# First MLP: relu transposed by VectorE blocks and ScalarE quarter copies, GpSimd issues the modulation pieces; both MLPs take the relu behind the fifth split

## The chip, the cores and the metric

The kernel runs on one core of a Trainium2 chip. The metric is the device time of one execution in microseconds. Before the change the median of three runs is 2226.82 us (2226.66 to 2227.34). Engines: TensorE (PE, with PEld for its weight loads), VectorE (DVE), ScalarE (ACT), GpSimd (POOL), SyncE (SP).

## The reference

Two transformer layers over a sequence of 256 tokens, model width 2048, in float32. Layer 0 mixes tokens by differential attention, layer 1 by sliding-window attention; each is followed by a squared-ReLU MLP of width 8192. Scale, shift and gate of each of the four sub-layers are computed from one conditioning vector c.

```python
def squared_relu_mlp(h, w_up, w_down):
    return jnp.square(jax.nn.relu(h @ w_up)) @ w_down

    c_act = jax.nn.silu(c)
    for i in range(DEPTH):
        mod = (c_act @ w_ada[i] + b_ada[i])[:, None, :]
        sh_a, sc_a, g_a, sh_m, sc_m, g_m = jnp.split(mod, N_MOD, axis=-1)
        h = x * (1.0 + sc_a) + sh_a
        ...
        x = layer_norm(ALPHA * x + (1.0 + g_a) * y, ln_mix_g[i], ln_mix_b[i])
        h = x * (1.0 + sc_m) + sh_m
        y = squared_relu_mlp(h, w_up[i], w_down[i])
        x = layer_norm(ALPHA * x + (1.0 + g_m) * y, ln_mlp_g[i], ln_mlp_b[i])
```

## The kernel before

**Blocks, subtiles, splits.** All weights are streamed once. A block is one product of 256 tokens by a 2048 x 512 piece of weights. SP loads it in four quarters of 1 MB into five slots `raw`. A block is worked off in 8 subtiles of 256 weight rows each. For a subtile ScalarE rounds the weights to float32r (`w_hi`, L528, `split_hi`), VectorE takes the rest (`w_lo = raw - w_hi`, L901, `split_lo`, written over `raw`), and TensorE does 12 matmuls: w_hi with the high part of the activations, w_lo with the high part, w_hi with the low part (L1709 to L1711), into `pair[:, b % 2]` in PSUM. Work on one subtile's weights by ScalarE and VectorE is called split n here, n from 0 to 7. `w_hi` has 6 slots, so split n of a block waits until TensorE has finished the subtile six before it (`used`); `pair` has two halves, so a block's result must have left PSUM before the second block after it starts.

**The MLPs.** Each MLP is four quarters of the width of 8192. A quarter is four up blocks (h into 512 columns each of w_up, with relu and square behind them) and four down blocks (f into w_down, added up in `y`); 32 blocks in each MLP. The order on each engine is written out by hand: `block_` runs over the 8 splits and calls at given numbers what else stands beside them: `before` (behind split `at`), `later` (behind its split), `hooks` and, on VectorE, `ada_tile` for the pieces. The work on the result of an up block stands in the block behind it, on all engines.

**The relu, its transpose and the square.** An up block's result has tokens on the partitions, the down product needs features there. In the first MLP ScalarE takes the relu from PSUM into `R` behind split 1 (`up_relu`, L553), TensorE turns `R` with eight transposes into `turn[:, 0]` in PSUM behind its subtile 1 (`turn_up`, `turn_tile`, L1603), ScalarE squares it twice from there behind split 4 (L560 into `SQ`, L561 rounded into `f_hi`), and VectorE takes the rest behind split 4 (`up_lo`, L1031, `f_lo`). In the second MLP (`ON_CHIP`), ScalarE's relu stands behind split 2, VectorE turns `R` with 16 transposes of 32 x 256, eight behind split 2 and eight behind split 3 (`up_turn_half`, L1040), each of which also moves its blocks to other partitions, ScalarE squares twice behind split 5 (L572, L573) and VectorE takes the rest behind split 5 (L1057). The first down block of a quarter waits for three `f_lo` at its start and for the fourth at its subtile 6.

**The modulation.** `c_act @ w_ada` is done on VectorE: a piece is 128 x 1024 of w_ada (0.5 MB), multiplied by one number per partition and added to `acc` (L929; L926 for the first of a sum). 16 pieces make a sum, which TensorE then adds over the partitions (L1627 or L1638). The first MLP carries 192 pieces, six or seven in each of 28 blocks, behind splits 0, 1, 3, (4,) 5, 6, 7 (`MLP_ADA`); the second 32. Pieces have four slots `ada_w`. SP issues them (`load_ada`, L374) between the weight quarters (`load_raw`, L397), in one queue; a piece waits until VectorE has used the one four before it, a quarter until TensorE has used the slot. In the first four blocks behind each norm VectorE also applies the norm's gain and bias to `x` (`affine`, L1311, L1312) behind split 7. GpSimd does the `rstd` powers, and clears `y` before the first block's result is needed (L1581); VectorE waits for that at the start of the MLP's second block.

## Time and profile before

| | |
|---|---|
| median of 3 runs | 2226.82 us (2226.66 to 2227.34) |
| the profiled execution | 2228.67 us, span 2226.9 us |
| TensorE busy | 2168.5 us, 97% of the span, granted clock 0.993 on average |
| VectorE busy | 1790.6 us, 80% |
| ScalarE busy | 981.3 us, 44% |
| GpSimd busy | 33.4 us, 2% |
| chain that ended last | TensorE 88%, VectorE 7% |
| moved by DMA | 596.41 MB, 268 GB/s on average |

The first MLP lies between about 495 and 1226 us of the span, the second between 1502 and the end. Matmuls overlap, so a matmul's own duration (0.39 us) is not its share of the time: their starts stand 0.2265 us apart. In the same way an instruction of ScalarE or VectorE can begin a little before the one in front of it has ended; where a step is spoken of, it is from start to start.

### The profile page before, as it was taken

Reading aid. Unit: us, or ns where it says so; the run is one execution under the profiler, and the core shown is the slowest. Engines: PE = TensorE matmul, PEld = TensorE weight load, DVE = VectorE, ACT = ScalarE, POOL = GpSimd, SP = SyncE. Lnnn points to the kernel's source line nnn. Section 1 sums busy time; section 2 is a strip of 40 time slices with the busy share of each in tenths; the row PEclk is TensorE's granted clock in tenths of the full one; section 3 lists DMA queues with packets and bytes.
Section 4 is the critical chain, followed back from the end, with each engine's and each line's share of the span. In section 5 each row is a group of like instructions: output and inputs, shape, how many; then the busy total and the mean of one; then the engine's idle time right before and its main releaser. Section 6 shows DMA issues by size and latency. Waiting matters only on the chain.

```text
span 2226.9 us, 26022 instructions
## 1 busy us (share of the span) xinstructions
PE 2168.5 (97%) x9952; PEld 1791.8 (80%) x9952; DVE 1790.6 (80%) x2057; ACT 981.3 (44%) x1330; POOL 33.4 (2%) x53
## 2 busy tenths in 40 slices
PE   6999999999999999999999999999999999999997
PEld 6887888877888888888888788777888888888886
DVE  6899998887997897888786888777966865874877
ACT  1135444546433443443353655536534443443441
POOL 0001000000000000000000000000000000000000
PEclk9899999999999999999999999999999999999999
DMA  9999888877999999999985643365766676666663
GB/s 360 384 331 347 322 320 300 306 245 256 361 364 325 354 366 335 325 380 350 323 311 190 198 152 119 122 207 190 236 221 223 213 241 206 219 217 219 228 234 113
DMA packets 262592, 596.41 MB, mean 268 GB/s; under 512 B 13426, under 2 KB 14788, under 8 KB 262468
## 3 DMA queue, kind: packets, MB, share of 16 engines
q1 hardware_dynamic: 254800, 579.45, 74.2%
q10 hardware_dynamic: 7668, 15.30, 2.2%
q8 instruction: 79, 1.29, 0.2%
q14 instruction: 45, 0.37, 0.0%
HBM read 592.60 MB, written 2.10 MB: 267 GB/s over the span
## 4 chain that ended last, share of the span: by engine, by line
PE 88%; DVE 7%; DMA 1%; issue 1%; ACT 1%; SPq 0%; DVEq 0%; POOL 0%; ACTq 0%; POOLq 0%
PE pair L1709 25%; PE pair L1711 25%; PE pair L1710 25%; DVE acc L916 2%; DVE w_lo L901 1%; PE pair L1967 1%; PE pair L1969 1%; PE pair L1968 1%; PE pair L1729 1%; PE pair L1731 1%; PE pair L1730 1%; PE turn L2041 1%; DMA y<-in_w_ada_dram 1%; PE turn L2022 1%; PE turn L1603 1%
## 5 line engine op out<-in xcount | busy, mean ns | idle before, releaser
L528 ACT ACTIVATE w_hi<-raw 128x1024 fp32r<-128x1024 f32 x712 | 726.8, 1056 | 620.2 <-PE pair L1711 297.4
L901 DVE TENSOR_TENSOR w_lo<-raw,w_hi 128x1024 fp32r<-128x1024 f32 x712 | 852.5, 1220 | 117.0 <-ACT w_hi L528 110.8
L1709 PE MATMUL pair<-w_hi,h_hi 128*128 128x512 f32 x1456 | 581.3, 399 | 1.5 <-DVE w_lo L901 0.8
L1711 PE MATMUL pair<-w_hi,h_lo 128*128 128x512 f32 x1456 | 567.8, 390 | 0.0
L1710 PE MATMUL pair<-w_lo,h_hi 128*128 128x512 f32 x1456 | 567.3, 390 | 0.0
L1709 PE MATMUL pair<-w_hi,f_hi 128*128 128x512 f32 x1056 | 414.0, 392 | 0.1
L1711 PE MATMUL pair<-w_hi,f_lo 128*128 128x512 f32 x1056 | 411.1, 389 | 0.0
L1710 PE MATMUL pair<-w_lo,f_hi 128*128 128x512 f32 x1056 | 410.9, 389 | 0.0
L929 DVE SCALAR_TENSOR_TENSOR acc<-ada_w,cvec,acc 128x1024 f32<-128x1024 f32 x300 | 383.6, 1279 | 1.8 <-DVE x L1312 0.9
L1709 PEld LDWEIGHTS pair<-w_hi,h_hi 128*128 128x128 f32 x1456 | 273.5, 188 | 62.9 <-DVE w_lo L901 6.3
L1711 PEld LDWEIGHTS pair<-w_hi,h_lo 128*128 128x128 f32 x1456 | 273.2, 188 | 58.4
L1710 PEld LDWEIGHTS pair<-w_lo,h_hi 128*128 128x128 f32 x1456 | 273.7, 188 | 55.5 <-issue 1.2
L1709 PEld LDWEIGHTS pair<-w_hi,f_hi 128*128 128x128 f32 x1056 | 198.2, 188 | 43.7 <-DVE w_lo L901 2.1
L1710 PEld LDWEIGHTS pair<-w_lo,f_hi 128*128 128x128 f32 x1056 | 198.3, 188 | 41.7 <-issue 1.0
L1711 PEld LDWEIGHTS pair<-w_hi,f_lo 128*128 128x128 f32 x1056 | 198.2, 188 | 41.5
L1040 DVE STREAM_TRANSPOSE work<-work 32x256 f32<-32x256 f32 x256 | 111.6, 436 | 55.7 <-ACT work L553 52.2
L553 ACT ACTIVATE work<-pair 128x1024 f32<-128x1024 f32 x32 | 32.9, 1029 | 222.3 <-PE pair L1711 222.3
L1066 DVE TENSOR_TENSOR y<-pair,y 128x1024 f32<-128x1024 f32 x30 | 36.7, 1224 | 101.2 <-PE pair L1711 101.2
L572 ACT ACTIVATE work<-work 128x1024 f32<-128x1024 f32 x16 | 17.0, 1062 | 90.7 <-DVE work L1040 90.7
L1967 PE MATMUL pair<-w_hi,f_hi 128*128 128x512 f32 x128 | 53.6, 419 | 1.9 <-DVE f_lo L1513 1.9
L1969 PE MATMUL pair<-w_hi,f_lo 128*128 128x512 f32 x128 | 50.1, 391 | 0.0
L1968 PE MATMUL pair<-w_lo,f_hi 128*128 128x512 f32 x128 | 49.9, 390 | 0.0
(190 smaller groups left out, 1669.5 us busy)
## 6 DMA issues: line engine op xcount, KB each, us to landing
ada_w<-in_w_ada_dram SPq DMA_DIRECT2D x320, 512.0 KB, 6.1
raw<-in_w_up_dram SPq DMA_DIRECT2D x128, 1024.0 KB, 6.1
raw<-in_w_down_dram SPq DMA_DIRECT2D x128, 1024.0 KB, 5.2
raw<-in_a_w_qkv_dram SPq DMA_DIRECT2D x48, 1024.0 KB, 7.6
ada_f<-in_w_ada_dram SPq DMA_DIRECT2D x44, 512.0 KB, 11.5
raw<-in_b_w_qkv_dram SPq DMA_DIRECT2D x20, 1024.0 KB, 5.2
raw<-in_a_w_o_dram SPq DMA_DIRECT2D x16, 1024.0 KB, 6.5
raw<-in_b_w_o_dram SPq DMA_DIRECT2D x16, 1024.0 KB, 5.1
```

Of the source, the lines that this page charges most:

```text
L528: act.activation(w_hi[:, (b.n * SUB + n) % SPLITS], raw[:, slot, k:k + 2], ACT.Copy).then_inc(hi_ready, 1)
L901: dve.tensor_tensor(w_lo[:, slot, k:k + 2], raw[:, slot, k:k + 2], w_hi[:, (b.n * SUB + n) % SPLITS].bitcast(F32), ALU.subtract).then_inc( ...
L916: ins = dve.scalar_tensor_tensor(dst, src, cvec[:, n % KT:n % KT + 1], dst, ALU.mult, ALU.add)
L929: ins = dve.scalar_tensor_tensor(acc[:, half], src, cvec[:, kt:kt + 1], acc[:, half], ALU.mult, ALU.add)
L1040: ins = dve.transpose(by_token(rows32(up_rows(RR), c), a), by_feature(rows32(up_rows(R), a), c))
L1066: dve.tensor_tensor(cols(y, j), pair[:, pp], cols(y, j), ALU.add).then_inc(evacuated, 1)
L1709: pe.matmul(o, hi[:, kt, at], w[:, k], start=kt == 0, stop=False)
L1710: pe.matmul(o, hi[:, kt, at], wl[:, k], start=False, stop=False)
L1711: mm = pe.matmul(o, lo[:, kt, at], w[:, k], start=False, stop=kt == KT - 1)
L1967: pe.matmul(o, f_hi[:, kt, at], w[:, k], start=kt == 0, stop=False)
L1968: pe.matmul(o, f_hi[:, kt, at], wl[:, k], start=False, stop=False)
L1969: mm = pe.matmul(o, f_lo[:, kt, at], w[:, k], start=False, stop=kt == KT - 1)
```

## The change

In the first MLP the relu is no longer turned by TensorE (`ON_CHIP` now holds both layers). VectorE turns `R` with one transpose of 128 x 1024 in blocks of 32 x 32 into `turn[:, 0]` in PSUM (`up_turn`), and ScalarE moves the blocks to their places with 16 copies of 32 x 256 from PSUM into `RR`, eight behind split 5 and eight behind split 6 (`up_move`), and then squares twice from `RR`; VectorE's rest stands behind split 6. The relu stands behind split 4 in both MLPs; in the second the 16 transposes follow it in one run. The 192 pieces of the first MLP are issued by GpSimd with semaphores of their own (`pool_arrived`): four behind the first rstd, the others behind the clearing of `y`, each as soon as its slot is free. SP issues only the weights there. What stood behind ScalarE's split 6 in the up blocks (`load_affine`) stands behind split 7.

```diff
--- before.py
+++ after.py
@@ -56,7 +56,8 @@
 
 MASKED = -1e30
 
-ON_CHIP = (1,)
+ON_CHIP = (0, 1)
+BY_SCALAR = (0,)
 
 T0_FIRST = 2
 T0_B = T0_FIRST + 16 + (0 if 0 in ON_CHIP else 4 * QUARTERS)
@@ -103,6 +104,7 @@
 UNITS_B = HB
 UNIT_AT_B = {8 * (50 + i) + 3 + k: 8 * i + k for i in range(NCH) for k in range(8)}
 MLP_HALVES = (12, 2)
+POOL_PIECES = MLP_HALVES[0] * KT
 MLP_GATE = (8, 0)
 READY = 6
 
@@ -275,6 +277,7 @@
         evacuated = sem("evacuated")
         ada_arrived = [sem(f"ada_arrived{i}") for i in range(ADA_SLOTS)]
         pre_arrived = [sem(f"pre_arrived{i}") for i in range(PRE_SLOTS)]
+        pool_arrived = [sem(f"pool_arrived{i}") for i in range(ADA_SLOTS)]
         ada_added = sem("ada_added")
         piece_taken = sem("piece_taken")
         x_turned = sem("x_turned")
@@ -487,8 +490,7 @@
                     return lambda q: w_rows(w_down[layer], f * D + q * 4 * P, j * NC)
 
                 load_block(up(0, 0))
-                parts = [(1, 0), (1, 1), (1, 3), (1, 4), (0, 5), (1, 2)] if layer == 0 else [(1, 5)]
-                tiles = iter([ada_src(l, part, half, kt) for l, part in parts for half in range(2) for kt in range(KT)])
+                tiles = iter([ada_src(1, 5, half, kt) for half in range(2) for kt in range(KT)])
 
                 def of():
                     return next(tiles)
@@ -496,9 +498,10 @@
                 for b in range(8 * QUARTERS - 1):
                     it, i = b // 8, b % 8
                     src = up(it, i + 1) if i < 3 else down(it, i - 3) if i < 7 else up(it + 1, 0)
-                    load_block(src, mlp_pieces(b, 2 * len(parts)), of)
+                    load_block(src, mlp_pieces(b, MLP_HALVES[layer]) if layer == 1 else (), of)
 
             mlp(0)
+            st.ada.n += POOL_PIECES
 
             for j in (4, 0, 1, 2, 3):
                 load_block(lambda q: w_rows(b_w_qkv[0], q * 4 * P, j * NC))
@@ -561,6 +564,20 @@
                     act.activation(f_hi[:, 4 * j:4 * j + 4], T[0], ACT.Square).then_inc(t_free[0], 1)
                     st.t0.n += 1
                     st.up.n += 1
+                return run
+
+            def up_move(first, last, then=None):
+
+                def run():
+                    act.wait_ge(up_blocks, st.turned.n + 1)
+                    for i in range(first, last):
+                        a, c = i // 4, i % 4
+                        ins = act.activation(by_token(rows32(up_rows(RR), c), a),
+                                             by_feature(rows32(turn[:, 0], a), c), ACT.Copy)
+                    if last == 16:
+                        ins.then_inc(up_moved, 1)
+                    if then:
+                        then()
                 return run
 
             def up_square_there(j):
@@ -806,8 +823,14 @@
                         hk[0] = load_last_rows
                     if layer in ON_CHIP:
                         if i < 4:
-                            hk[5] = up_square_there(i)
-                        block_(before=up_relu if i < 4 else None, hooks=hk, at=2)
+                            late = hk.pop(6, None)
+                            if late:
+                                hk[7] = late
+                            if layer in BY_SCALAR:
+                                hk[5], hk[6] = up_move(0, 8), up_move(8, 16, up_square_there(i))
+                            else:
+                                hk[5] = up_square_there(i)
+                        block_(before=up_relu if i < 4 else None, hooks=hk, at=4)
                         continue
                     block_(before=up_relu if i < 4 else None, later=(4, up_square(i)) if i < 4 else None, hooks=hk)
 
@@ -921,7 +944,14 @@
                 a = st.ada
                 kt, half = a.n % KT, (a.n // KT) % 2
                 src = ada_w[:, a.n % ADA_SLOTS]
-                dve.wait_ge(ada_arrived[a.n % ADA_SLOTS], a.at(1 - PRE // ADA_SLOTS, 16, over=ADA_SLOTS))
+                turns = (a.n - PRE) // ADA_SLOTS + 1
+                before = 3 * 2 * KT // ADA_SLOTS
+                if turns <= before:
+                    dve.wait_ge(ada_arrived[a.n % ADA_SLOTS], 16 * turns)
+                elif turns <= before + POOL_PIECES // ADA_SLOTS:
+                    dve.wait_ge(pool_arrived[a.n % ADA_SLOTS], 16 * (turns - before))
+                else:
+                    dve.wait_ge(ada_arrived[a.n % ADA_SLOTS], 16 * (turns - POOL_PIECES // ADA_SLOTS))
                 if kt == 0:
                     ins = dve.tensor_scalar(acc[:, half], src, cvec[:, 0:1], None, ALU.mult)
                 else:
@@ -1033,21 +1063,18 @@
                     st.t0.n += 1
                 return run
 
-            def up_turn_half(first):
-
-                for i in range(first, first + 8):
-                    a, c = i // 4, i % 4
-                    ins = dve.transpose(by_token(rows32(up_rows(RR), c), a), by_feature(rows32(up_rows(R), a), c))
-                return ins
+            def up_turn(b, pp):
+
+                dve.wait_ge(evacuated, b + 3)
+                dve.transpose(turn[:, 0], up_rows(R)).then_inc(up_blocks, 1)
 
             def up_turn_across(b, pp):
 
                 dve.wait_ge(evacuated, b + 3)
-                up_turn_half(0)
-
-            def up_turn_rest():
-
-                up_turn_half(8).then_inc(up_moved, 1)
+                for a in range(4):
+                    for c in range(4):
+                        ins = dve.transpose(by_token(rows32(up_rows(RR), c), a), by_feature(rows32(up_rows(R), a), c))
+                ins.then_inc(up_moved, 1)
 
             def up_rest(j):
 
@@ -1470,8 +1497,7 @@
                     if b < NCH:
                         hooks[7] = affine(site, b)
                     if layer in ON_CHIP and i < 4:
-                        hooks[3] = up_turn_rest
-                        block_(before=up_turn_across, later=(5, up_rest(i)), ada=mlp_pieces(b, halves), hooks=hooks)
+                        block_(before=up_turn if layer in BY_SCALAR else up_turn_across, later=(6 if layer in BY_SCALAR else 5, up_rest(i)), at=4, ada=mlp_pieces(b, halves), hooks=hooks)
                         continue
                     block_(before=(down_last if last else down_add)(i - 4) if i >= 4 else None,
                            later=(4, up_lo(i)) if i < 4 else None, ada=mlp_pieces(b, halves), hooks=hooks)
@@ -1577,8 +1603,22 @@
                 link(pool.tensor_tensor(sm[:, 7, 1:2], sm[:, 4, 0:1], sm[:, 3, 0:1], ALU.add))
                 power(sm[:, 7, 0:1], sm[:, 7, 1:2], orstd_ready)
             site(1)
+            parts = [(1, 0), (1, 1), (1, 3), (1, 4), (0, 5), (1, 2)]
+            tiles = iter([ada_src(l, part, half, kt) for l, part in parts for half in range(2) for kt in range(KT)])
+            st.ada.n = PRE + 3 * 2 * KT
+
+            def load_ada(n):
+
+                a = st.ada
+                for _ in range(n):
+                    pool.wait_ge(ada_added, a.at(1))
+                    pool.dma_start(ada_w[:, a.n % ADA_SLOTS], next(tiles)).then_inc(pool_arrived[a.n % ADA_SLOTS], 16)
+                    a.n += 1
+
+            load_ada(ADA_SLOTS)
             pool.wait_ge(h_ready, 28)
             pool.memset(y[:], 0.0).then_inc(y_clear, 1)
+            load_ada(POOL_PIECES - ADA_SLOTS)
             site(2)
 
             pool.wait_ge(h_ready, 36)
```

ScalarE, first MLP, from the first block's last splits to the first up block's squares and the splits behind them (`pair` is the PSUM result, `work` holds `R`, `RR` and `SQ`, `turn` is PSUM). Before:

```order
L528 ACTIVATE w_hi<-raw 128x1024 x4
L553 ACTIVATE work<-pair 128x1024
L528 ACTIVATE w_hi<-raw 128x1024 x3
L560 ACTIVATE work<-turn 128x1024
L561 ACTIVATE f_hi<-turn 128x1024
L528 ACTIVATE w_hi<-raw 128x1024 x5
```

After:

```order
L531 ACTIVATE w_hi<-raw 128x1024 x7
L556 ACTIVATE work<-pair 128x1024
L531 ACTIVATE w_hi<-raw 128x1024
L575 ACTIVATE work<-turn 32x2x4x32 x8
L531 ACTIVATE w_hi<-raw 128x1024
L575 ACTIVATE work<-turn 32x2x4x32 x8
L589 ACTIVATE work<-work 128x1024
L590 ACTIVATE f_hi<-work 128x1024
L531 ACTIVATE w_hi<-raw 128x1024 x6
```

The relu (L553, now L556) stands behind split 4 where it stood behind split 1, and 16 copies (L575) stand between split 5 and the squares, with split 6 among them.

VectorE, first MLP, the block behind the first up block, from split 2 on. Before:

```order
L901 TENSOR_TENSOR w_lo<-raw,w_hi 128x1024 x2
L929 SCALAR_TENSOR_TENSOR acc<-ada_w,cvec,acc 128x1024
L901 TENSOR_TENSOR w_lo<-raw,w_hi 128x1024
L1031 TENSOR_TENSOR f_lo<-work,f_hi 128x1024
L901 TENSOR_TENSOR w_lo<-raw,w_hi 128x1024
L929 SCALAR_TENSOR_TENSOR acc<-ada_w,cvec,acc 128x1024
L901 TENSOR_TENSOR w_lo<-raw,w_hi 128x1024
L929 SCALAR_TENSOR_TENSOR acc<-ada_w,cvec,acc 128x1024
L901 TENSOR_TENSOR w_lo<-raw,w_hi 128x1024
L1311 TENSOR_TENSOR x<-x,bc 128x2x512
L1312 TENSOR_TENSOR x<-x,bc 128x2x512
```

After:

```order
L924 TENSOR_TENSOR w_lo<-raw,w_hi 128x1024 x2
L959 SCALAR_TENSOR_TENSOR acc<-ada_w,cvec,acc 128x1024
L924 TENSOR_TENSOR w_lo<-raw,w_hi 128x1024
L1069 STREAM_TRANSPOSE turn<-work 128x1024
L924 TENSOR_TENSOR w_lo<-raw,w_hi 128x1024
L959 SCALAR_TENSOR_TENSOR acc<-ada_w,cvec,acc 128x1024
L924 TENSOR_TENSOR w_lo<-raw,w_hi 128x1024
L1084 TENSOR_TENSOR f_lo<-work,f_hi 128x1024
L959 SCALAR_TENSOR_TENSOR acc<-ada_w,cvec,acc 128x1024
L924 TENSOR_TENSOR w_lo<-raw,w_hi 128x1024
L1338 TENSOR_TENSOR x<-x,bc 128x2x512
L1339 TENSOR_TENSOR x<-x,bc 128x2x512
```

The block transpose (L1069) stands behind split 4, and `f_lo` (L1031, now L1084), which waits for ScalarE's squares, moves from behind split 4 to behind split 6; pieces, split 7 and the sums on `x` stand behind it.

VectorE, second MLP, from the last splits of the first block to the first `f_lo`. Before:

```order
L901 TENSOR_TENSOR w_lo<-raw,w_hi 128x1024 x5
L1040 STREAM_TRANSPOSE work<-work 32x2x4x32 x8
L901 TENSOR_TENSOR w_lo<-raw,w_hi 128x1024
L1040 STREAM_TRANSPOSE work<-work 32x2x4x32 x8
L901 TENSOR_TENSOR w_lo<-raw,w_hi 128x1024 x2
L1057 TENSOR_TENSOR f_lo<-work,f_hi 128x1024
```

After:

```order
L924 TENSOR_TENSOR w_lo<-raw,w_hi 128x1024 x7
L1076 STREAM_TRANSPOSE work<-work 32x2x4x32 x16
L924 TENSOR_TENSOR w_lo<-raw,w_hi 128x1024
L1084 TENSOR_TENSOR f_lo<-work,f_hi 128x1024
L956 TENSOR_SCALAR acc<-ada_w,cvec 128x1024
```

The 16 transposes (L1040, now L1076) stand together behind split 4 of their block, where they stood behind splits 2 and 3.

## Rows read from the trace of the kernel before

**Rows 1.** the page's chain that ended last, shares of the span by engine.

```profile
PE 88%; DVE 7%; DMA 1%; issue 1%; ACT 1%; SPq 0%; DVEq 0%; POOL 0%; ACTq 0%; POOLq 0%
```

**Rows 2.** busy time by stretch: length, engines with counts, clock, DMA, GB/s.

```profile
523.90:704.33 180.43, 180.43 (x825) 149.95 (x824) 159.81 (x141) 75.12 (x76) 0.00 (x0) 1.00 0.97 349
1530.81:1706.07 175.26, 175.26 (x769) 143.84 (x768) 131.75 (x153) 76.42 (x76) 0.00 (x0) 1.00 0.68 225
```

**Rows 3.** timeline of VectorE, second MLP: start, duration, instruction, idle before.

```profile
1640.79 1.22 DVE L1066 TENSOR_TENSOR y<-pair,y 128x1024 f32<-128x1024 f32 x1 [5.78 <-PE pair L1711]
...
1684.31 1.23 DVE L1066 TENSOR_TENSOR y<-pair,y 128x1024 f32<-128x1024 f32 x1 [5.78 <-PE pair L1711]
```

**Rows 4.** timeline of TensorE around one relu's transposes, first MLP.

```profile
732.03 0.39 PE L1711 MATMUL pair<-w_hi,h_lo 128*128 128x512 f32 x1
732.27 1.03 PE L1603 MATMUL turn<-ident,work 128*128 128x128 f32 x8
...
733.84 0.39 PE L1709 MATMUL pair<-w_hi,h_hi 128*128 128x512 f32 x1
```

**Rows 5.** timeline of TensorE, second MLP, at subtile 4 of an up block.

```profile
1541.26 0.39 PE L1711 MATMUL pair<-w_hi,h_lo 128*128 128x512 f32 x1
1541.62 0.50 PE L1709 MATMUL pair<-w_hi,h_hi 128*128 128x512 f32 x1
```

**Rows 6.** timelines of ScalarE and VectorE, second MLP, behind a quarter's fourth up block.

```profile
1596.97 1.03 ACT L553 ACTIVATE work<-pair 128x1024 f32<-128x1024 f32 x1 [5.78 <-PE pair L1711]
...
1606.50 1.06 ACT L572 ACTIVATE work<-work 128x1024 f32<-128x1024 f32 x1 [5.67 <-DVE work L1040]
1607.47 1.04 ACT L573 ACTIVATE f_hi<-work 128x1024 fp32r<-128x1024 f32 x1
...
1602.88 3.59 DVE L1040 STREAM_TRANSPOSE work<-work 32x256 f32<-32x256 f32 x8
1606.50 2.36 DVE L901 TENSOR_TENSOR w_lo<-raw,w_hi 128x1024 fp32r<-128x1024 f32 x2
```

**Rows 7.** groups by form: busy us, mean ns | idle before, releaser.

```profile
L1040 DVE STREAM_TRANSPOSE work<-work 32x256 f32<-32x256 f32 x256 | 111.6, 436 | 55.7 <-ACT work L553 52.2
...
L926 DVE TENSOR_SCALAR acc<-ada_w,cvec 128x1024 f32<-128x1024 f32 x20 | 14.9, 747 | 0.0
...
L528 ACT ACTIVATE w_hi<-raw 128x1024 fp32r<-128x1024 f32 x712 | 726.8, 1056 | 620.2 <-PE pair L1711 297.4 <-DMA raw<-in_w_down_dram 120.5 <-DMA raw<-in_a_w_qkv_dram 95.7
...
L846 ACT ACTIVATE work<-turn,small 128x256 f32<-128x256 f32 x32 | 14.9, 470 | 18.9 <-DVE small L1497 18.9
...
L749 ACT ACTIVATE y<-turn 128x256 f32<-128x256 f32 x8 | 3.1, 384 | 19.8 <-PE turn L1907 19.8
L603 ACT ACTIVATE y<-pair 64x512 f32<-64x512 f32 x4 | 2.4, 594 | 2.5 <-PE pair L1669 2.4
```

**Rows 8.** timeline of ScalarE: two copies onto other partitions, three w_hi.

```profile
1265.19 1.20 ACT L603 ACTIVATE y<-pair 64x512 f32<-64x512 f32 x2 [1.51 <-PE pair L1669]
...
705.26 2.94 ACT L528 ACTIVATE w_hi<-raw 128x1024 fp32r<-128x1024 f32 x3
```

**Rows 9.** timeline of VectorE in the first MLP's second and third block.

```profile
519.83 1.23 DVE L901 TENSOR_TENSOR w_lo<-raw,w_hi 128x1024 fp32r<-128x1024 f32 x1 [1.35 <-POOL y L1581]
...
533.34 1.22 DVE L901 TENSOR_TENSOR w_lo<-raw,w_hi 128x1024 fp32r<-128x1024 f32 x1
534.47 1.28 DVE L929 SCALAR_TENSOR_TENSOR acc<-ada_w,cvec,acc 128x1024 f32<-128x1024 f32 x1
535.67 1.22 DVE L901 TENSOR_TENSOR w_lo<-raw,w_hi 128x1024 fp32r<-128x1024 f32 x1
...
539.14 1.22 DVE L1311 TENSOR_TENSOR x<-x,bc 128x1024 f32<-128x1024 f32 x1
...
541.83 1.28 DVE L929 SCALAR_TENSOR_TENSOR acc<-ada_w,cvec,acc 128x1024 f32<-128x1024 f32 x1 [0.21 <-DVE x L1312]
```

**Rows 10.** DMA issues from 550 to 1200 us: count, size, median us to landing.

```profile
ada_w<-in_w_ada_dram SPq DMA_DIRECT2D x180, 512.0 KB, 6.6
```

## The prediction

> **What bounds the kernel now.** I read the page's chain first: TensorE holds 88% of the chain that ended last, VectorE 7% [rows 1]. The table of stretches says how close the others are: in the first MLP, between the first relu and the fifth (eight blocks on, 523.9 to 704.33), TensorE is busy for all 180.43 us at full granted clock, VectorE for 159.81 (89%), ScalarE for 75.12, and the DMA engines are at 0.97; in the same stretch of the second MLP VectorE has 131.75 of 175.26 and the DMA 0.68 [rows 2]. A TensorE instruction taken out of an MLP shortens the run by its own length, as long as nobody else comes late, and in the first MLP VectorE has little to give.
>
> The unit is a subtile, 12 matmuls. Without anything between them a block of 8 takes 21.76 us: two additions into y that stand two blocks apart start at 1640.79 and 1684.31 [rows 3]; that is 2.72 us per subtile. ScalarE and VectorE may run 6 subtiles ahead. Below, T is the moment at which TensorE ends an up block, about 0.2 us before its relu starts. In the block that follows, TensorE asks for split n (0 to 7) at T + 2.72n.
>
> **First MLP: what goes.** From the matmul at 732.03 to the one at 733.84 pass 1.81 us, where four steps of 21.76 / 96 = 0.227 are 0.91; eight transposes of the relu lie between [rows 4]. That is 0.90. The stretch agrees: 180.43 - 8 x 21.76 = 6.35, which is seven times 0.90, four relus and three modulation sums (these stay). 16 relus: 16 x 0.90 = **14.4 us** out, all on the path.
>
> **Second MLP: what the later relu gives.** TensorE has no transposes there, and yet the eight blocks take 175.26 us against 174.08, 0.295 for each of four relus [rows 2]. It is a short wait: the matmuls at 1541.26 and 1541.62 stand 0.36 apart instead of 0.23, and the pair behind them is nearly as far apart [rows 5]. The cause, read in another block: relu at 1596.97, then eight transposes, split 3, eight more transposes from 1602.88, and split 4 only at 1606.50, done 1.22 later at 1607.72, when TensorE asks at 1596.77 + 10.88 = 1607.65 [rows 6]. With the relu behind split 4 that split is done before T. The 16 transposes then run from T+1.3 to T+8.5, split 5 to T+9.7 (asked at T+13.6), f_lo, behind two squares (0.97 + 1.04), to T+11.8 (its first reader comes at T+16.3, the seventh subtile of the first down block), split 6 to T+13 (asked at T+16.3). Nothing is late: 16 x 0.295 = **4.7 us** out.
>
> **First MLP: what comes in.** Per up block:
> VectorE: one block transpose 128x1024, SBUF to PSUM, in no row. Nearest are the 128x1024 subtraction, 1.22 us [rows 6], and the 32x256 transpose, 0.436; the fastest vector operation of this size takes 0.75 [rows 7], four of the small transposes in a row 1.8. I take 1.23, since from 256 to 1024 columns a vector operation gains about 0.8.
> ScalarE: 16 copies of 32x256, PSUM to SBUF. A 128x256 copy from PSUM takes 0.384 [rows 7]. What counts is their step. ScalarE normally lets two of its instructions overlap: three w_hi of 1.056 end in 2.94, not 3.17. But the two 64x512 copies that change their partitions take 1.20 for two of 0.594: no overlap [rows 7, 8]. VectorE does the same: its eight 32x256 transposes, each onto other partitions, take 3.59, or 0.449 each, over 0.436 [rows 6, 7]. All 16 copies change the partitions they write. I take 0.395 each, 6.3 us; the ends are 0.28 (full overlap) and 0.47, a 128x256 activation with a pointer operand [rows 7].
> The Trainium skill (VectorE: DVE Perf Modes, "Two Vector instructions with no wait between them") says that a vector instruction whose output starts in another group of 32 partitions waits for all earlier ones; the 0.449 agrees. The same notes (ScalarE: Activation LUTs, "What ACT_TABLE_LOAD costs") say that ScalarE instructions back to back overlap by about 93 ns and name no exception; by that the step would be an estimated 0.29, and the two 64x512 copies contradict it. It is the first rival's case.
>
> On ScalarE's account alone (75 of 180 us) or VectorE's (16 x 1.2 more) this would be hidden beside the matmuls. But **VectorE stands in a chain.** From the start of the transpose: 1.27 to ScalarE, 8 copies 3.16, w_hi 0.94 (its step in [rows 8]), 8 copies 3.16, squares 0.03 + 0.97 + 1.04, 0.03 back: f_lo can start 10.6 us later. VectorE has in that time the transpose, one or two pieces and two splits, 4.6 to 5.8 us, and then stands still in front of f_lo, with the pieces and the next splits queued behind it. After f_lo (1.14) come, up to the next transpose, six splits at 1.14 and five pieces at 1.20 (steps as in [rows 9]), 14.0 us. One round is 10.6 + 14.0 = **24.6 us against TensorE's 21.76**: 2.8 lost per up block. In the first four blocks the affine sums on x stand in it too, 539.14 to 541.83, 2.69 us [rows 9]: a round of 27.3, 5.5 lost.
>
> How much is forgiven? Split 7 is done 10.6 + 1.14 + 1.20 + 1.22 = 14.2 after the transpose starts and asked at T+19.0; f_lo of the fourth chunk is done after 11.8 and asked at T+16.3. So the transpose may start at T+4.5.
> First quarter: T is 523.7. VectorE starts the next block's splits at 519.83, held by the clearing of y [rows 9]; split, piece (the first of a sum, 0.66), split, piece, three splits with a piece between them bring its transpose to 528.6, T+4.9. Three rounds later it would be at T+21.4: 16.9 us of TensorE waiting, and the sums of the fourth block add 1.9 (next block's first split at 4.5 + 19.2 = T+23.7 against T+21.8). Some **19 us**.
> Quarters 2 to 4: the down blocks need 8 x 1.14 + 7 x 1.20 + 1.14 = 18.7 of 21.76, so the lead is back. Transposes at T+1.3, 4.1, 6.9, 9.7 against 4.5: 5.2 lost. Three times: **15.6 us**.
> Waits added: 34.6.
>
> **Pieces.** SP no longer issues them in the first MLP; its 128 weight quarters go out as slots come free, so ScalarE's waits for weights should shrink; none of them costs anything today. GpSimd's queue is otherwise idle (its four rstd powers of this part and the clearing of y come before or after; four issues stand ahead of the clearing). A piece takes 6.6 us from issue to landing now [rows 10]; in VectorE's densest run it comes back to a slot after 4 x 2.34 - 1.28 = 8.1 us. No row shows a load issued by GpSimd; up to 1.5 us more is hidden. I take nothing.
>
> **Sum.** 34.6 - 14.4 - 4.7 = +15.5 us. The profiled run took 2228.67 with a span of 2226.9; the median is 2226.82. I put the difference on the median: **2242 us**. A hundredth of a microsecond on the copies' step is 0.16 on each of 12 rounds and four limits, 2.6 us: from 0.375 to 0.42 it is 2237 to 2249, at 0.47 it is 2262. The transpose at 0.75 takes 8 off, at 1.8 it adds 9.
>
> **Rivals.**
> A. ScalarE overlaps the copies: step 0.29 to 0.31. The chain is 8.9, rounds are 25.6 and 22.9, the transpose may start at T+6.2. First quarter 4.9 + 3 x 3.85 - 6.2 = 10.3 plus 2; later quarters reach 1.3 + 3 x 1.15 = 4.7 and lose nothing. 12.3 - 19.1 = -7, 2220; at 0.31 about 2223. The sign turns at a step of 0.335 (15.5 / 2.6 hundredths below mine). Most rows of ScalarE speak for it, the only one with changing partitions against it.
> B. Pieces come late. DMA share is 0.97 where the pieces are densest [rows 2], and another queue then competes with SP's. If a piece takes 9.6 us, VectorE loses about 1.5 at every fourth piece while it is the bound, that is in some 10 of the 48 fours: +15, 2257. It decides from a landing of 8.1 us.
> C. TensorE never waits, because VectorE's idle time covers the chain: 2226.8 - 19.1 = 2207.7. Against it: VectorE's 89%, with only 20.6 us idle in eight blocks.
>
> **Numbers.** Main case 0.66 (2234 to 2251), A 0.17 (2218 to 2224), B 0.12 (2251 to 2265), C 0.05. A measurement here tells 0.2% (4.5 us) from no change. Faster by more: C and two thirds of A, 0.16. Within: the rest of A, and 0.03 for a main case much smaller than worked out, 0.09. Slower: 0.75. The range leaves out C, the lower edge of A and the upper end of B: 2220 to 2260.
>
> **What would show it.** No eight-fold transposes in the first MLP; in the second, relus of one quarter 21.76 apart. In the first MLP's rows a 32x256 copy step of 0.39 (A: 0.29); VectorE waiting 4 us or more for f_hi in each up block; TensorE waiting for w_lo and f_lo, 19 us in the first quarter, most at splits 7 and 0, and about 5 in each later one; its relus over 27 us apart at the start. For B: VectorE waiting for DMA, landing over 8 us. I am wrong if the copies overlap, if the block transpose is far from 1.2, or if VectorE's queue has more lead than I gave it.

## The result, and the profile after

| | before | after |
|---|---|---|
| median | 2227.08 us (2226.66 to 2228.34) | 2253.58 us (2251.09 to 2256.0) |
| ratio | | 1.0116, 95% interval 1.0104 to 1.0128 |
| the profiled execution | 2228.67, span 2226.9 | 2251.09, span 2249.3 |
| TensorE / VectorE / ScalarE / GpSimd busy | 2168.5 / 1790.6 / 981.3 / 33.4 | 2161.5 / 1809.8 / 1085.7 / 137.7 |

Slower by 26.5 us, 22.4 between the two profiled spans. The page after, beginning with the busy times, then the chain that answers [rows 1] and the copies' group:

```profile
PE 2161.5 (96%) x9824; PEld 1783.4 (79%) x9824; DVE 1809.8 (80%) x2073; ACT 1085.7 (48%) x1586; POOL 137.7 (6%) x245
...
PE 77%; DVE 13%; ACT 4%; issue 4%; DMA 2%; SPq 0%; ACTq 0%; DVEq 0%; POOL 0%; POOLq 0%
...
L575 ACT ACTIVATE work<-turn 32x256 f32<-32x256 f32 x256 | 96.3, 376 | 88.0 <-DVE turn L1069 85.0
```

TensorE's share of the chain fell from 88% to 77%, VectorE's rose from 7% to 13%, ScalarE's from 1% to 4%. TensorE's own busy time is only 7 us lower although 16 x 0.90 of transposes are gone: part of what is left runs slower (below).

VectorE in the block behind the first up block, from the block transpose on (start, duration, instruction, idle before):

```profile
527.14 1.25 DVE L1069 STREAM_TRANSPOSE turn<-work 128x1024 f32<-128x1024 f32 x1
528.30 1.20 DVE L924 TENSOR_TENSOR w_lo<-raw,w_hi 128x1024 fp32r<-128x1024 f32 x1
529.42 1.25 DVE L959 SCALAR_TENSOR_TENSOR acc<-ada_w,cvec,acc 128x1024 f32<-128x1024 f32 x1
532.60 1.23 DVE L924 TENSOR_TENSOR w_lo<-raw,w_hi 128x1024 fp32r<-128x1024 f32 x1 [1.93 <-ACT w_hi L531]
537.77 1.23 DVE L1084 TENSOR_TENSOR f_lo<-work,f_hi 128x1024 fp32r<-128x1024 f32 x1 [3.94 <-ACT f_hi L590]
...
554.41 1.25 DVE L1069 STREAM_TRANSPOSE turn<-work 128x1024 f32<-128x1024 f32 x1
```

And ScalarE in the same time:

```profile
528.42 3.08 ACT L575 ACTIVATE work<-turn 32x256 f32<-32x256 f32 x8 [4.03 <-DVE turn L1069]
531.51 1.06 ACT L531 ACTIVATE w_hi<-raw 128x1024 fp32r<-128x1024 f32 x1
532.60 3.10 ACT L575 ACTIVATE work<-turn 32x256 f32<-32x256 f32 x8
535.73 1.06 ACT L589 ACTIVATE work<-work 128x1024 f32<-128x1024 f32 x1
536.70 1.04 ACT L590 ACTIVATE f_hi<-work 128x1024 fp32r<-128x1024 f32 x1
```

This is the chain of the prediction, row by row: from the transpose at 527.14 over 16 copies, one w_hi and two squares to f_lo at 537.77, 10.63 us, of which VectorE stands still for 1.93 + 3.94. The next transpose comes at 554.41, a round of 27.27 where TensorE needs 21.76. TensorE in turn waits for VectorE (waits of the whole span: total, times, longest):

```profile
PE pair L1749 <- DVE w_lo L924: 20.7, 12, 3.0
PE pair L1749 <- DVE f_lo L1084: 8.9, 4, 3.0
```

The starts of ScalarE's relu (L553 before, L556 after) show where the time goes. From each quarter's first relu to the next quarter's, the 0.90 of each relu's transposes taken off before:

| first MLP | before, without transposes | after | lost | lost, by TensorE's block ends |
|---|---|---|---|---|
| quarter 1 | 180.43 - 3.6 | 197.70 (522.42 to 720.12) | 20.9 | 19.9 |
| quarter 2 | 180.47 - 3.6 | 185.37 (to 905.49) | 8.5 | 9.5 |
| quarter 3 | 181.31 - 3.6 | 185.11 (to 1090.60) | 7.4 | 6.1 |
| quarter 4, up to the second MLP's first relu | 464.70 - 3.6 | 467.35 (to 1557.95) | 6.3 | 7.6 |

The last column is the better one for a single quarter: it goes from the end of the last matmul of the first up block (522.38, 719.10, 905.45 and 1089.22) and not from the relu. Two relus of the changed kernel start late behind that end, by 1.0 and 1.4 us (720.12 and 1090.60), where in the kernel before all start within 0.04 of it. The relu now stands behind ScalarE's split 4, and when one of the 1 MB loads of weights lands late, the split and the relu behind it are late too. TensorE's last matmul of the block, and ScalarE:

```profile
718.71 0.39 PE L1751 MATMUL pair<-w_hi,h_lo 128*128 128x512 f32 x1
...
719.03 1.06 ACT L531 ACTIVATE w_hi<-raw 128x1024 fp32r<-128x1024 f32 x1 [4.22 <-DMA raw<-in_w_up_dram]
720.12 1.03 ACT L556 ACTIVATE work<-pair 128x1024 f32<-128x1024 f32 x1
```

Lost 43.1 in all by either column, 14.4 back for the transposes, and the first relu itself came 1.5 earlier (522.42 against 523.90): 27.1. That 1.5 is not the change's: in the profiles of all fourteen kernels of this document the first relu starts between 522.06 and 524.57, and at 522.34 in second_late (below), where nothing ahead of it was changed. The second MLP gives 4.7 back, which leaves 22.4 (from its first relu to the end of the span 696.1 before and 691.4 after; 4.4 of it up to the last relu). The first relus of its first two quarters are now eight bare blocks apart, without the 1.18 us of [rows 2]:

```profile
1557.95:1732.03 174.08, 174.08 (x769) 144.19 (x768) 133.31 (x155) 77.35 (x76) 0.00 (x0) 1.00 0.68 227
```

**What no step of the prediction had: half clock.** TensorE around the wait that ends at 573.69, in the first quarter:

```profile
571.31 0.39 PE L1751 MATMUL pair<-w_hi,h_lo 128*128 128x512 f32 x1
573.69 0.50 PE L1749 MATMUL pair<-w_hi,h_hi 128*128 128x512 f32 x1 [1.99 <-DVE w_lo L924]
574.02 0.54 PE L1750 MATMUL pair<-w_lo,h_hi 128*128 128x512 f32 x1
574.35 0.63 PE L1751 MATMUL pair<-w_hi,h_lo 128*128 128x512 f32 x1
574.78 0.63 PE L1749 MATMUL pair<-w_hi,h_hi 128*128 128x512 f32 x1
...
577.34 0.49 PE L1749 MATMUL pair<-w_hi,h_hi 128*128 128x512 f32 x1
577.67 0.40 PE L1750 MATMUL pair<-w_lo,h_hi 128*128 128x512 f32 x1
```

The same time by stretches (the granted clock is the third number from the end):

```profile
574.00:576.00 2.00, 2.00 (x6) 1.57 (x5) 2.00 (x3) 0.00 (x0) 0.54 (x1) 0.53 1.02 365
576.00:578.00 2.00, 2.00 (x7) 1.57 (x6) 2.00 (x2) 0.00 (x0) 0.54 (x1) 0.62 0.94 332
578.00:580.00 2.00, 2.00 (x11) 1.64 (x10) 2.00 (x3) 0.00 (x0) 0.00 (x0) 1.00 1.00 370
```

Right behind the wait (2.38 us from start to start) matmul starts stand 0.43 apart instead of 0.227, at a granted clock of 0.53 (1.2 GHz and not 2.4), for seven steps. There are six such stretches in the first MLP, 44 steps of 0.2 us, 8.8 us in all, each behind a wait; before there is none. That does not make them 8.8 us of the loss: in the first quarter TensorE goes on to wait for VectorE behind each of its three stretches (the last of these waits, of 2.36, ends at 629.90), so they only shorten the next wait. The three stretches of the later quarters (8, 7 and 6 steps, 4.2 us) stand behind the quarter's last wait and come on top.

### The profile page after: what moved, and what is told of

Same layout as the page of the kernel before. It is cut to its first block, busy times and chain, and to the rows that moved or that the text cites. A ratio compares the mean times of both kernels' runs of the same rounds, so it can differ in the third digit from the quotient of the medians.

```text
span 2249.3 us, 26022 instructions
## 1 busy us (share of the span) xinstructions
PE 2161.5 (96%) x9824; PEld 1783.4 (79%) x9824; DVE 1809.8 (80%) x2073; ACT 1085.7 (48%) x1586; POOL 137.7 (6%) x245
## 4 chain that ended last, share of the span: by engine, by line
PE 77%; DVE 13%; ACT 4%; issue 4%; DMA 2%; SPq 0%; ACTq 0%; DVEq 0%; POOL 0%; POOLq 0%
PE pair L1749 22%; PE pair L1751 22%; PE pair L1750 22%; DVE w_lo L924 2%; DVE acc L959 2%; DVE acc L939 2%; ACT work L575 2%; PE pair L2007 1%; PE pair L2009 1%; PE pair L2008 1%; PE pair L1769 1%; DMA ada_f<-in_w_ada_dram 1%; PE pair L1771 1%; PE pair L1770 1%; PE turn L2081 1%
## 5 line engine op out<-in xcount | busy, mean ns | idle before, releaser
L1749 PE MATMUL pair<-w_hi,f_hi 128*128 128x512 f32 x1056 | 416.4, 394 | 13.9 <-DVE f_lo L1084 8.9
L1751 PE MATMUL pair<-w_hi,f_lo 128*128 128x512 f32 x1056 | 413.5, 392 | 0.0
L1750 PE MATMUL pair<-w_lo,f_hi 128*128 128x512 f32 x1056 | 413.4, 392 | 0.0
L575 ACT ACTIVATE work<-turn 32x256 f32<-32x256 f32 x256 | 96.3, 376 | 88.0 <-DVE turn L1069 85.0
L1615 POOL DMA_DIRECT2D ada_w<-in_w_ada_dram x192 | 103.8, 541 | 546.5 <-DVE acc L959 510.3
L1076 DVE STREAM_TRANSPOSE work<-work 32x256 f32<-32x256 f32 x256 | 111.6, 436 | 19.7 <-ACT work L556 16.4
L1084 DVE TENSOR_TENSOR f_lo<-work,f_hi 128x1024 fp32r<-128x1024 f32 x32 | 39.2, 1225 | 76.2 <-ACT f_hi L590 76.2
L589 ACT ACTIVATE work<-work 128x1024 f32<-128x1024 f32 x32 | 34.0, 1062 | 104.6 <-DVE work L1076 104.1
L1587 POOL TENSOR_TENSOR rstd<-rstd,minus_half 128x1 f32<-128x1 f32 x8 | 4.7, 594 | 1094.7 <-DVE rstd L1192 1094.7
```

Of the source, the lines that this page charges most:

```text
L575: ins = act.activation(by_token(rows32(up_rows(RR), c), a), by_feature(rows32(turn[:, 0], a), c), ACT.Copy)
L1076: ins = dve.transpose(by_token(rows32(up_rows(RR), c), a), by_feature(rows32(up_rows(R), a), c))
L1084: dve.tensor_tensor(f_lo[:, 4 * j:4 * j + 4], chunk(SQ), f_hi[:, 4 * j:4 * j + 4].bitcast(F32), ALU.subtract).then_inc(f_ready, 1)
L1615: pool.dma_start(ada_w[:, a.n % ADA_SLOTS], next(tiles)).then_inc(pool_arrived[a.n % ADA_SLOTS], 16)
L1749: pe.matmul(o, hi[:, kt, at], w[:, k], start=kt == 0, stop=False)
L1750: pe.matmul(o, hi[:, kt, at], wl[:, k], start=False, stop=False)
```

## The experiments

**One part at a time.** First the second MLP alone:

```diff
-                        block_(before=up_relu if i < 4 else None, hooks=hk, at=2)
+                        block_(before=up_relu if i < 4 else None, hooks=hk, at=4)
...
                 up_turn_half(0)
+                up_turn_half(8).then_inc(up_moved, 1)
...
-                        hooks[3] = up_turn_rest
-                        block_(before=up_turn_across, later=(5, up_rest(i)), ada=mlp_pieces(b, halves), hooks=hooks)
+                        block_(before=up_turn_across, later=(5, up_rest(i)), at=4, ada=mlp_pieces(b, halves), hooks=hooks)
```

> The kernel before with one part of the change alone: in the second MLP the relu stands behind split 4 and the 16 transposes follow it in one run. My theory: the short waits of TensorE (16 of 0.295 us) go, so 4.7 us less than before, about 2222.3; the relus of one quarter of the second MLP stand 21.76 apart. Rival: the gain seen in the second MLP of the changed kernel (relus there 4.4 us closer together) came from its later start or from the rest of the change; then this kernel takes as long as before, 2227.

2222.54 us (2222.01 to 2225.08; before 2227.31): ratio 0.9978 (0.9969 to 0.9987), 4.8 us less, and the relus 21.76 apart (1529.41, 1551.17, 1572.93, 1594.69). The 4.7 stand by themselves.

Then GpSimd's issuing alone: kernel before, with the change's `load_ada` on GpSimd and its waits on `pool_arrived`, and SP's pieces of the first MLP taken out.

> The kernel before with one part of the change alone: GpSimd issues the 192 pieces of the first MLP, everything else as before. My theory: nothing, 2227 within 2 us, since in the changed kernel a piece landed after 6.8 us against 6.6 and VectorE waited 1.3 us for them in all. Rival: a second queue beside the one for the weights delays the weights or the pieces where the DMA engines are at 0.97, and part of the changed kernel's loss is its; then 5 to 15 us more than before.

2228.3 (2226.87 to 2229.43), ratio 1.0004 (0.9994 to 1.0014): nothing. Issues of this kernel (KB, median us to landing):

```profile
raw<-in_w_up_dram SPq DMA_DIRECT2D x128, 1024.0 KB, 5.5
...
ada_w<-in_w_ada_dram POOLq DMA_DIRECT2D x192, 512.0 KB, 6.7
```

So the whole loss, and more, is the first MLP's new way of turning, with the place of its relu.

**The order on VectorE: f_lo later.**

```diff
-                        block_(before=up_turn if layer in BY_SCALAR else up_turn_across, later=(6 if layer in BY_SCALAR else 5, up_rest(i)), at=4, ada=mlp_pieces(b, halves), hooks=hooks)
+                        rest = up_rest(i)
+                        if layer in BY_SCALAR:
+                            first = hooks.get(7)
+                            hooks[7] = lambda first=first, rest=rest: (first and first(), rest())
+                        block_(before=up_turn if layer in BY_SCALAR else up_turn_across,
+                               later=None if layer in BY_SCALAR else (5, rest), at=4, ada=mlp_pieces(b, halves), hooks=hooks)
```

> The changed kernel with f_lo of the first MLP behind VectorE's split 7 (behind the two sums on x where there are any) instead of split 6, nothing else. My theory (VectorE stands still in front of f_lo while ScalarE copies and squares, and the splits queued behind it come late): split 7, a piece and the sums now lie in that time. Rounds from transpose to transpose are 10.6 + 1.1 + five splits of 1.14 + three pieces of 1.2 = 21 to 22.3 us without sums, up to 22.9 with them, against 27.3 in the changed kernel. Later quarters lose nothing (1.3 + 3 x 0.5 = T+2.8 against T+4.5), the first about 3 us; 2227 - 14.4 - 4.7 + 3 = 2211, with up to 2 more for a lower clock. Rival: VectorE has too much work in the up blocks whatever its order (8 splits, 7 pieces, a transpose, f_lo and sums are 19.9 to 22.6 us of 21.76 and the copies hold ScalarE); then the order changes a few us and it stays above 2240.

2259.56 (2257.66 to 2261.95), ratio 1.0145 (1.013 to 1.016): worse than the changed kernel by 6, where I expected 42 less. VectorE of this kernel, the block behind the first up block:

```profile
540.50 1.23 DVE L924 TENSOR_TENSOR w_lo<-raw,w_hi 128x1024 fp32r<-128x1024 f32 x1 [3.69 <-ACT w_hi L531]
541.64 1.22 DVE L1338 TENSOR_TENSOR x<-x,bc 128x1024 f32<-128x1024 f32 x1
542.89 1.23 DVE L1339 TENSOR_TENSOR x<-x,bc 128x1024 f32<-128x1024 f32 x1
544.27 1.23 DVE L1084 TENSOR_TENSOR f_lo<-work,f_hi 128x1024 fp32r<-128x1024 f32 x1
```

ScalarE of this kernel at that time:

```profile
534.38 3.10 ACT L575 ACTIVATE work<-turn 32x256 f32<-32x256 f32 x8
537.51 1.06 ACT L589 ACTIVATE work<-work 128x1024 f32<-128x1024 f32 x1
538.48 1.04 ACT L590 ACTIVATE f_hi<-work 128x1024 fp32r<-128x1024 f32 x1
539.42 5.79 ACT L531 ACTIVATE w_hi<-raw 128x1024 fp32r<-128x1024 f32 x6
```

The wait in front of f_lo is gone, and the same 3.7 us stand in front of split 7: its w_hi is queued behind copies and squares on ScalarE, where I had looked at VectorE's queue alone. The sums and f_lo came behind that, so f_lo came 15.35 after the transpose, and TensorE waited for it at subtile 6 of the first down block, up to 5.6 us. My theory had the right chain and the wrong queue; the rival (too much work on VectorE) was not yet excluded.

**The order on both engines.** As above, and on ScalarE:

```diff
-                                hk[5], hk[6] = up_move(0, 8), up_move(8, 16, up_square_there(i))
+                                last, late = hk.get(7), up_square_there(i)
+                                hk[6] = up_move(0, 8)
+                                hk[7] = up_move(8, 16, lambda last=last, late=late: (late(), last and last()))
```

> The changed kernel with ScalarE's order changed too: the first eight copies behind its split 6, the last eight and the squares behind its split 7, and f_lo on VectorE behind split 7 (behind the sums on x). My new theory, from the run with f_lo moved alone: there VectorE stood still in front of split 7 instead (3.7 us), because w_hi of split 7 stands behind the copies and squares in ScalarE's queue; the chain that binds goes through ScalarE's queue, not through f_lo's place alone. With split 7 ahead of the last copies VectorE's wait is what is left of 10.6 us after transpose, three splits and two or three pieces (and sums): 2.4 to 3.6 us, or none with sums. Rounds of 22.2 to 22.6 us. First quarter about 3 us of TensorE's waiting, later ones none (T+2.8 at the fourth transpose): 2227 - 19.1 + 3 = 2211, to 2214 with a stretch at lower clock. Rival (VectorE has too much work in up blocks, whatever the order): above 2240.

2220.6 (2216.74 to 2221.34), ratio 0.9965 (0.9952 to 0.9978): 33 less than the changed kernel with the same instructions in another order, so the order it was, not the amount of work. It stays 9.6 above my 2211. Rows of this kernel's second quarter, ScalarE and then VectorE:

```profile
711.52 1.06 ACT L531 ACTIVATE w_hi<-raw 128x1024 fp32r<-128x1024 f32 x1 [4.06 <-DMA raw<-in_w_up_dram]
712.50 3.06 ACT L575 ACTIVATE work<-turn 32x256 f32<-32x256 f32 x8
```

```profile
706.63 1.25 DVE L1071 STREAM_TRANSPOSE turn<-work 128x1024 f32<-128x1024 f32 x1
...
721.83 1.23 DVE L1086 TENSOR_TENSOR f_lo<-work,f_hi 128x1024 fp32r<-128x1024 f32 x1 [3.94 <-ACT f_hi L590]
```

TensorE's four waits for f_lo are 8.1 us, two of them followed by half clock (2.6 us). One, of 2.6, is the first quarter's that I expected. In quarter 2 the weights came late, and the copies, which now stand behind split 6, came late with them: 15.2 us from transpose to f_lo instead of 10.6, carried on to the fourth f_lo.

**Less work, the same order.** The sums on x moved from the first four to the next four blocks (f_lo still behind split 6):

```diff
-                    hk = {6: load_affine(b + 1)} if b in (1, 2) else {}
+                    late = 4 if layer == 0 else 0
+                    hk = {6: load_affine(b - late + 1)} if b - late in (1, 2) else {}
...
-                    if b < NCH:
-                        hooks[7] = affine(site, b)
+                    late = 4 if layer == 0 else 0
+                    if 0 <= b - late < NCH:
+                        hooks[7] = affine(site, b - late)
```

> The changed kernel with the two sums on x of each of the first four blocks of the first MLP moved four blocks on, into the down blocks; f_lo stays behind split 6. My theory: the rounds of the first quarter shrink by 2.7 us from 27.3 to 24.6; VectorE's last up block of the quarter has no sums behind it; the waits of TensorE in the first quarter fall from 13.7 us to about 4, and its stretches at half clock there (23 matmul steps, 4.6 us) go nearly all. The later quarters keep their waits (7.6, 4.3, 5.8). About 13 us less than the changed kernel, 2240. Rival: the sums cost the changed kernel nothing because the chain over ScalarE hides them; then 2253 again.

2244.38 (2241.91 to 2247.37), ratio 1.0077 (1.0062 to 1.0092): 9.2 less. The rounds did what they should; its transposes of the first quarter:

```profile
528.02 1.26 DVE L1070 STREAM_TRANSPOSE turn<-work 128x1024 f32<-128x1024 f32 x1
...
552.59 1.26 DVE L1070 STREAM_TRANSPOSE turn<-work 128x1024 f32<-128x1024 f32 x1
...
601.71 1.26 DVE L1070 STREAM_TRANSPOSE turn<-work 128x1024 f32<-128x1024 f32 x1
```

24.57, 24.56, 24.56 (the third transpose starts at 577.15): the 24.6 of the prediction. By TensorE's block ends quarter 1 loses 9.0 instead of 19.9. But in the down blocks the sums took the lead that VectorE builds up there: quarter 2's first transpose starts 5.7 us behind its relu (709.22, transpose 714.88), where the changed kernel's came 2.2 behind the end of TensorE's block (719.10, transpose 721.27). The price in TensorE's time is smaller: quarters 2 to 4 lose 10.5, 7.1 and 6.3 where the changed kernel's lose 9.5, 6.1 and 7.6. 10.9 gained, 0.7 given back, and a first relu that starts 0.9 later: 9.2.

**The copies' price.** Two copies of 64x512 in the place of the 16; half of the values stay where they were, so this kernel leaves that part of the computation out:

```diff
-                    for i in range(first, last):
-                        a, c = i // 4, i % 4
-                        ins = act.activation(by_token(rows32(up_rows(RR), c), a),
-                                             by_feature(rows32(turn[:, 0], a), c), ACT.Copy)
                     if last == 16:
+                        for i in range(2):
+                            ins = act.activation(up_rows(RR)[64 * i:64 * i + 64, 0:512], turn[64 * i:64 * i + 64, 0, 0:512], ACT.Copy)
                         ins.then_inc(up_moved, 1)
```

> The changed kernel with the 16 copies of 32x256 replaced by two of 64x512 (half of the data stays where it was, so this part of the computation is left out), 1.2 us in the place of 6.2 of ScalarE's queue; all else as in the changed kernel. My theory (the chain over ScalarE is what costs, VectorE's own work is the same): the chain from transpose to f_lo is 5.5 us, VectorE hardly stands still, rounds are about 20 us and with the sums 22.2; the waits of TensorE and the stretches at half clock go, 2208 to 2211. Rival (VectorE's transpose, which fills VectorE from 89% up, is what costs): still above 2235.

2209.74 (2209.12 to 2209.99), ratio 0.9919 (0.9904 to 0.9934). VectorE does all it does in the changed kernel, transpose and sums too, and TensorE no longer waits for it in the MLP. Its first transpose stands at 529.14, f_lo at 534.66: a chain of 5.5. So 44 of the changed kernel's microseconds hang on some 5 us of ScalarE's queue, 16 times, and VectorE's 1.2 us a relu cost nothing.

**The other way round: all on VectorE.** `BY_SCALAR = ()`.

> The changed kernel with the first MLP's relu turned in the second MLP's way: 16 transposes of 32x256 on VectorE (7.2 us), no copies on ScalarE, f_lo behind split 5. My theory: ScalarE's chain is short (the squares, 2.1 us), but VectorE itself is over the block's time: 8 splits 9.1, 7 pieces 8.4, transposes 7.2, f_lo 1.1 = 25.8 us of 21.76, 28.5 with the sums, plus a wait of about 1 us for f_hi. The first quarter loses about 20 us, each later one about 9: with 19.1 off that is some 30 us more than before, 2257, a few more for half clock, and TensorE's waits are nearly all for w_lo. Rival: the chain through ScalarE was all that cost, then about 2208.

2270.51 (2269.68 to 2272.9), ratio 1.0194 (1.0179 to 1.0209). Its waits of TensorE, whole span:

```profile
PE pair L1749 <- DVE w_lo L924: 42.5, 29, 3.8
```

Rounds are 28.20 and 28.50 (transposes at 526.83, 555.03, 583.53), as added up, nearly all the waits are for w_lo, and the total is 13 above my sum, part of it half clock (68 steps, 13.6 us, in the first MLP). VectorE can be the bound by its work alone; in the changed kernel it is not.

**The copies' order.** `a, c = i % 4, i // 4` in `up_move`.

> The changed kernel with ScalarE's 16 copies in another order: four in a row write the same 32 partitions of RR and read four different groups of turn, where the changed kernel writes another group with each copy and reads one group four times. Nothing else. My theory (two ScalarE instructions overlap unless the second writes other partitions): 12 of 16 steps fall from 0.386 to about 0.29, the 16 copies from 6.2 to 5.0 us, the chain by 1.2, and with 3 rounds and one limit in each quarter the time by 10 to 18 us, to about 2240. Rival: copies never overlap there, or it is the group read that counts: 2253 again.

2251.86 (2250.68 to 2252.66), ratio 1.0107 (1.0092 to 1.0122): 1.7 less, inside the spread of both. I had expected 2240; the step is what it was:

```profile
528.03 3.10 ACT L575 ACTIVATE work<-turn 32x256 f32<-32x256 f32 x8 [4.00 <-DVE turn L1069]
```

(3.10 - 0.376) / 7 = 0.389. These copies do not overlap, and it is not the changing partitions of the output that prevents it: my reason for the number was wrong, the number right. That an overlap needs both sides to stay in one group is not excluded: in either order one side changes, here what the copies read.

**TensorE stopped on purpose.** In the kernel before, second MLP; the loop is GpSimd's, `pause` is a hook of TensorE behind subtile n:

```diff
+PAUSES = {4: {2: 6}, 9: {2: 6, 3: 6}, 12: {2: 6, 4: 6}, 17: {2: 6, 4: 6, 6: 6}, 20: {2: 12}, 22: {2: 3, 3: 3}, 25: {2: 6, 5: 6}}
...
+            for b, at in PAUSES.items():
+                for n, k in at.items():
+                    pool.wait_ge(used, SPLITS + SUB * (PAUSE_BLOCK + b) + n + 1)
+                    for _ in range(k):
+                        link(pool.memset(rope_a[:], 0.0))
+                    pool.sem_inc(paused, 1)
...
+            def pause():
+                count[0] += 1
+                pe.wait_ge(paused, count[0])
```

> The kernel before, with TensorE stopped on purpose in seven blocks of the second MLP, where otherwise it never stops: behind a subtile it waits for GpSimd, which does k small fills of 128x384 one after the other (about 0.4 to 0.5 us each). Block 4: once, k = 6. Block 9: after subtiles 2 and 3, k = 6 each. Block 12: after 2 and 4. Block 17: after 2, 4 and 6. Block 20: once, k = 12. Block 22: after 2 and 3, k = 3 each. Block 25: after 2 and 5. My theory: half clock comes of the waits themselves, so it is seen here too, some 1 to 3 us behind a pause, for about 8 steps of 0.43 instead of 0.227 (1.6 us), behind the close pairs and the long one, and not behind the short ones. Each pause costs its own length and 0.2 us more for each slow step, no more. Rival: the half clock of the changed kernel has to do with what ScalarE, VectorE or GpSimd did there (pieces issued by GpSimd, copies); then no slow step stands here.

2284.01 us in its one execution, span 2282.2: 55.3 above the span before. Its 13 pauses stand as gaps of 3.35 (ten), 6.20 (one) and 1.92 us (two) between starts, 40.6 us beyond a normal step; 64 steps at half clock are 12.8; together 53.4 of the 55.3. TensorE behind the second pause of block 9:

```profile
1748.76 0.79 PE L1718 MATMUL pair<-w_hi,h_hi 128*128 128x512 f32 x1 [2.96 <-POOLq L1599]
1749.35 0.63 PE L1719 MATMUL pair<-w_lo,h_hi 128*128 128x512 f32 x1
...
1751.49 0.47 PE L1718 MATMUL pair<-w_hi,h_hi 128*128 128x512 f32 x1
1751.80 0.40 PE L1719 MATMUL pair<-w_lo,h_hi 128*128 128x512 f32 x1
```

```profile
1749.00:1751.00 2.00, 2.00 (x5) 1.58 (x6) 1.47 (x2) 0.00 (x0) 0.00 (x0) 0.50 1.06 412
```

Half clock comes of TensorE's own standing still, here without any copies and with GpSimd doing nothing but the fill. Of ten pauses of 3.35 eight were followed at once by 5 to 8 slow steps, single ones too; the first of block 9 and the first of block 17 were not. The long one was followed by 12, the two short ones by none. Where they were followed by any, the ten pauses cost 1.3 us each on top of themselves (52 steps on eight). I had expected it of close pairs and the long one only.

**Both repairs together, and one step further.** split_first with the sums in the down blocks and the wait for the cleared y moved to block 4:

> The kernel split_first, and also the two sums on x of the first four blocks moved four blocks on into the down blocks, and VectorE's wait for the cleared y moved to the first down block, where y is first needed. My theory: nothing of the first quarter's loss is left, so TensorE waits nowhere in the first MLP: 2227 - 14.4 - 4.7 = 2208, granted clock never below full in it. Rival: a loss that has another cause (the first MLP's loads, the second queue) stays, 2212 or more.

2213.87 (2211.63 to 2215.84), ratio 0.9941 (0.9924 to 0.9958). By the number this is the rival's case, though the first quarter's loss is gone as expected and no stretch of the first MLP is at half clock: TensorE still waits for the fourth f_lo of each later quarter (0.65, 0.25 and 0.75), and its later quarters lose 0.9, 0.5 and 0.9. Then f_lo of the first three chunks behind split 0 of the next block:

```diff
                         rest = up_rest(i)
                         if layer in BY_SCALAR:
-                            first = hooks.get(7)
-                            hooks[7] = lambda first=first, rest=rest: (first and first(), rest())
+                            if i > 0:
+                                hooks[0] = up_rest(i - 1)
+                            if i == 3:
+                                hooks[7] = rest
```

> The kernel split_first_sums_down, with f_lo of the first three chunks of a quarter behind VectorE's split 0 of the next block, and only the fourth behind split 7. My theory: there rounds were 22.24 us by VectorE's wait of 1.1 to 3.6 in front of f_lo; now VectorE does not stand still there, its own work is 19.9 us of 21.76, and the transposes stand 21.76 apart. TensorE's last waits in the first MLP (about 2 us) go: 2208 to 2211, against 2213.9. Rival: no gain, since what is left of the difference to 2208 lies elsewhere (weights that arrive late, or the sums that stand in the down blocks).

2213.27 (2210.73 to 2215.99), ratio 0.9938 (0.9922 to 0.9955): no gain, the rival's case. VectorE does not stand still any more in front of the first three f_lo of the quarter, but it does, for 2.2 to 3.4 us in the first quarter, in front of the split just ahead of them, whose w_hi stands behind the copies and squares on ScalarE:

```profile
537.35 1.23 DVE L927 TENSOR_TENSOR w_lo<-raw,w_hi 128x1024 fp32r<-128x1024 f32 x1 [3.39 <-ACT w_hi L531]
```

The wait had moved once more, as in rest_behind_7, and the transposes stand 22.0 apart (525.76, 547.76, 569.76), not 21.76. That costs nothing in the first quarter, since three rounds of 0.24 too much are forgiven. From the first relu to the fifth TensorE is busy throughout, at full clock; before, this took 180.43 [rows 2]:

```profile
522.44:699.24 176.80, 176.80 (x793) 146.66 (x792) 162.69 (x144) 100.86 (x141) 28.58 (x53) 1.00 0.99 352
```

The 3.63 between them are the four transposes of relu, 3.6. And with SyncE issuing the pieces again, as before:

> The kernel float with its 192 pieces issued by SyncE between the weight quarters again, as in the kernel before; nothing else. Float takes 2213.3 (2210.7 to 2216.0) where 14.4 + 4.7 below the kernel before is 2208. Theory one: with VectorE this full the pieces and weights from two queues come late in some executions; SyncE's fixed order (one queue) takes that away: 2208 to 2210 with less spread. Theory two: who issues them makes nothing, as in the kernel before: 2213 again. Theory three: SyncE's order holds the weights behind pieces that wait for VectorE's slots, and now that VectorE is later in the up blocks this costs something: above 2216.

2212.8 (2211.59 to 2214.91), ratio 0.993 (0.9917 to 0.9944): the same within the spread. Both kernels beat the kernel before by about 15 us and the changed one by 40. The profiled execution of float has a span of 2208.9, 18.0 below that of before where 14.4 + 4.7 = 19.1 were to be had. But 1.5 of the 18.0 are again the first relu (522.44 against 523.90), so 2.6 of the first MLP's 14.4 are missing. The trace shows 2.2 of them as two waits of TensorE for the fourth f_lo, in quarters 3 and 4. These are ScalarE ahead of quarter 3, and then the first of the two waits:

```profile
878.91 1.06 ACT L531 ACTIVATE w_hi<-raw 128x1024 fp32r<-128x1024 f32 x1 [5.47 <-DMA raw<-in_w_up_dram]
...
960.68 0.47 PE L1761 MATMUL pair<-w_hi,f_hi 128*128 128x512 f32 x1 [0.93 <-DVE f_lo L1087]
```

The relu behind this split starts 3.7 us behind the end of TensorE's block, and the four transposes of the quarter are late with it. In float_sp the relus are at most 1.2 late, and its two waits are 0.3 each. So late weights are what is left to look at; no run takes them away alone. Float's other executions are 1 to 5 us longer, with a mean granted clock of 0.992 to 0.995; they have no trace, and where these microseconds go stays open.

## Why the prediction was right, point by point

- **What goes**: 14.4 for the transposes and 4.7 in the second MLP: measured 4.7 in the changed kernel and 4.8 alone; the transposes are confirmed by float's quarter, 3.63 for four.
- **Durations**: block transpose 1.23, measured 1.251; copies' step 0.395, measured 0.389 (0.386 in some runs of eight). The reason given, changing output partitions, was wrong (copies_grouped). The Trainium skill (ScalarE: Activation LUTs, "What ACT_TABLE_LOAD costs") gives about 93 ns of overlap for ScalarE instructions back to back; w_hi has it here (four of 1.05 end in 3.89, so 0.10 each), these copies show none.
- **The chain and the rounds**: 10.6 and 27.3, measured 10.63 and 27.27; without the sums 24.6, measured 24.56 (sums_in_down). Rival A fell with the step.
- **Forgiven until T+4.5, first transpose at T+4.9**: the transpose came 4.9 after T (527.14, relu 522.42).
- **First quarter 19**: measured 19.9 by TensorE's block ends. A reduce, shown in the next point, adds 1.3 to it, and TensorE's own part of that sum gives 0.9 back.
- **Later quarters 5.2 each, the mis-sized term**: measured 9.5, 6.1 and 7.6 by block ends, 23.1 instead of 15.6. Three things were left out. A modulation sum ends in every second or third block, and its reduce stands on VectorE in the chain's round, behind f_lo (in the first quarter at 620.72, between the fourth f_lo and split 7):

```profile
783.14 1.22 DVE L990 TENSOR_REDUCE mod<-turn 128x8 f32<-128x1024 f32 x1
784.39 0.17 DVE L991 TENSOR_TENSOR mod<-mod,bvec 128x8 f32<-128x8 f32 x1
```

  Rounds with it are 25.91 (771.36 to 797.27; 931.13 to 957.04), those without 24.57, one per quarter, and in quarter 4 the gate's sum stands there instead (1091.75 to 1117.75, 26.00). That is 1.3 to 1.4 each, of which TensorE's own part of the sum, 0.9 in the same blocks, gives some back; [rows 2] held the sums only as TensorE's time. The second is half clock, 1.2 to 1.6 a quarter. The third is ScalarE's wait for weights, which the prediction put at nothing because it costs nothing in the kernel before. With the relu behind split 4 it costs something: the relus at 720.12 and 1090.60 are 1.0 and 1.4 late, so the first transposes of quarters 2 and 4 come at T+2.3 and T+2.7 and not at T+1.3, and in quarter 2 a wait of 0.96 stands between the copies as well. By rounds, quarter 3: 24.58 + 25.91 + 24.05 (a block with a piece less) - 3 x 21.76 = 9.3, the transpose at T+1.3, 4.5 forgiven, 1.8 back for two of TensorE's own sums ahead of the fourth f_lo, 1.4 of half clock: 5.7, measured 6.1. Quarters 2 and 4 come out within 0.7 in the same way. The price of the late weights is read from rows; no run isolates it.
- **Pieces by GpSimd: nothing.** gpsimd_pieces shows it; landing was 6.9 us in the stretch of [rows 10] against 6.6, and in the changed kernel VectorE waited 1.3 us for pieces. Rival B fell.
- **Rival C** (TensorE never waits) would have been the outcome of another order of the same instructions, nearly: 2213.
- **Sum**: +15.5, measured +22.4 between the spans: 8.5 more by the terms above (43.1 lost instead of 34.6), 1.5 less by the earlier first relu, which was luck. Between the medians it is +26.5, 4.1 more: before's profiled execution lay 1.6 above its median, after's 2.5 below. The other executions of after show a mean granted clock of 0.988 to 0.989 where the profiled one has 0.990; why they differ by 5 us where before's differ by 1.7 is not explained.
- **The range**: 2253.58 is 11.6 above the 2242 worked out and just above the 2234 to 2251 of the main case. It lies in the stretch that was held for rival B, and B did not happen: the mechanism and most of its sizes were right, but that the stated range held the result is in part luck. Half clock, some 4 us of the loss, was in no case of the prediction.
- The prediction called the chain VectorE's. It is a loop over two queues, and the run that moved f_lo alone failed because of this.

## What to carry to other kernels

When work moves to an engine that is idle half the time, price the round, not the share: from the instruction that hands over to the one that takes back, over both queues, with everything queued behind either, against the time that the bound engine needs for one step. If the round is longer, look first for the place of the long stretch in its own queue: here the next split's rounding had to stand ahead of the second half of the copies, and f_lo behind the next work of VectorE, both together. Moving f_lo alone only shifted the wait; the other move alone was not run. An instruction that waits for one engine should also not be put behind another's wait without need: the relu behind split 4 came up to 3.7 us late in float when weights were late. And work put where an engine builds up its lead is in part paid for at the place where the lead was needed.

## What the hardware did that I had not expected

- TensorE's granted clock fell to half (1.2 GHz) behind many of its own stops, for 5 to 13 matmul steps. In pauses it did so behind eight of ten stops of 3.35 us (1.3 us each), behind one of 6.20 (2.4 us), behind none of two of 1.92. Where TensorE goes on to wait for another engine's round this is free, and behind the last wait of a series it is not.
- ScalarE's copies of 32x256 from PSUM follow each other in 0.389 us at a duration of 0.376, whether each writes another 32 partitions or four in a row write the same and read different ones, while its 128x1024 roundings of 1.06 follow in 0.94 to 0.97.
- Issuing 192 loads of 0.5 MB on GpSimd took 103.8 us of its time, 0.54 each, and they landed after 6.9 us where SyncE's took 6.6 in the same stretch.
